# The last projection by seven half-size products instead of eight, half of its weight sums made by accumulating DMAs

## The chip, the cores and the metric

The kernel runs on one core of a Trainium2 chip. The metric is the device time of one execution in microseconds (us); less is better. The kernel before has a median of 1404.72 us over 3 runs (1404.39 to 1404.82).

## The reference, cut to what matters

A decoder trunk of two layers over 512 tokens with 2048 features, all in float32. The second layer (pooling mixer) ends in the projection that is changed:

```python
def _odd_mixer(h, w_in, c_w, c_b, c_scale, w_out):
    p = h @ w_in
    v, z = jnp.split(p, 2, axis=-1)
    pooled = _causal_pool_means(v) - v
    ...
    g = jnp.einsum("bsgc,gcd->bsgd", g, c_w) + c_b
    y = g.reshape(bsz, s, W_C) * c_scale
    return (y * jax.nn.silu(z)) @ w_out        # (512 x 2048) @ (2048 x 2048)
...
x = x + _rmsnorm(y, o_norm_post[i])
```

## The kernel before, in words

Every float32 operand of a matrix product is split in a rounded part (`hi`, type float32r) and a rest (`lo`), and a product is three matmuls, hi·hi, hi·lo and lo·hi, 512 columns each (`product`, L417 to L419). The kernel is written out by hand: each engine has its own instruction list, and semaphores alone order them.

Weights come in slabs of 128 x 2048 (1 MB). SyncE (SP) loads a slab into one of two `raw` buffers (`load`, L253) as soon as VectorE (DVE) has made the rest of the slab before the last. ScalarE (ACT) rounds it into `w_hi` (L650), DVE subtracts and writes `w_lo` (L909), each into one of four slots; `split_ahead` does it three slabs ahead of the TensorE (PE), and a slot is free when PE has counted the slab four places earlier in `slab_done`. `lo_ready` counts finished slabs.

The end of the second layer goes like this. (1) Four groups of channels are mapped by a 512 x 512 matrix each (`o_cw`, one slab per group). GpSimd (POOL) makes the rests of the pooled tiles (L404), ACT rounds them (L849); DVE adds the bias and multiplies by the gate (`group`, L1197), ACT rounds the gated tiles (`mapped_rounded`, L873), DVE makes their rests (L1079). Even groups use PSUM banks 0 to 3, odd ones banks 4 to 7. (2) The last projection: 4 blocks of 512 output columns, each 4 slabs (4 feature tiles of 128 each); 4 tiles of 128 tokens per slab, so 16 products or 48 matmuls a slab, 768 matmuls in all. The tokens are the stationary operand, the weights move. (3) Behind a block ACT squares each token tile's bank with a sum (`y_squares`, L786) and DVE multiplies it by the gain into `rows` (L1105). The last block is done token tile by token tile; then DVE reduces the sums, POOL raises them to -1/2 (L375), DVE scales and adds the residual (L1128), and SP stores (L312, L315). The residual rows `x_mid` and the gain `o_post` are loaded ahead of the second block.

Of the kernel before, what the change touches and what calls it, by code (L numbers as in the profile page):

```python
# [20 lines left out]

# [49 lines left out]

A_X, A_B, A_C, A_Z, B_VAL, B_GATE, B_Z = (n * W_A for n in range(7))
# [13 lines left out]
def build(nc, x, x_t, vec, e_post, e_in, e_out, o_pre, o_post, o_in, o_cw, o_out, out):  # L86
    ctx = ExitStack()
    with ctx:
        def sb(name, shape, dt=F32):
            return ctx.enter_context(nc.sbuf_tensor(name, shape, dt))  # L90
# [4 lines left out]

        h_hi = sb("h_hi", [P, KT, T], F32R)
# [20 lines left out]
        diagonals = sb("diagonals", [P, TT, P])  # L117
# [9 lines left out]
        silu_z = scratch[:, :].rearrange("p (j t) -> p j t", j=KT)  # L127

# [67 lines left out]
        out_ready = sem("out_ready")  # L196

# [41 lines left out]
        def _(sp):  # L239
# [69 lines left out]
            token_major_loads(o_out, AT_O2, ((gain_post, o_post),), x_mid, 2 * KT)  # L309
            for t in range(TT - 1):  # L310
                sp.wait_ge(out_ready, 4 * t + 4)
                sp.dma_start(out[t * P:(t + 1) * P, :], tok[:, t, :]).then_inc(out_stored, 16)  # L312
            for j in range(4):
                sp.wait_ge(out_ready, 4 * (TT - 1) + j + 1)
                sp.dma_start(out[(TT - 1) * P:, j * T:(j + 1) * T],  # L315
                             part4(tok[:, TT - 1, :], j)).then_inc(out_stored, 16)
            sp.wait_ge(out_stored, 16 * (TT - 1 + 4))
# [3 lines left out]
        def _(pool):  # L321
# [84 lines left out]

            powers(POST1, TT)
# [3 lines left out]
        def _(pe):  # L411
# [231 lines left out]
        def _(act):  # L643
# [222 lines left out]

            def mapped_rounded(g):
                for m in range(4):
                    j = 4 * g + m
# [3 lines left out]
                    nc.scalar.activation(h_hi[:, j, :], rows[:, j, :], ACT.Copy)\  # L873
                        .then_inc(u_hi_ready, 1)

            for g in range(NG):
                if g > 0:
                    pooled_rounded(g)
                split_ahead(AT_O1C, g)
                if g > 0:  # L880
                    mapped_rounded(g - 1)
            mapped_rounded(NG - 1)

            post_sets = [POST1 + t for t in range(TT)]
            blocks(AT_O2, 1, post_sets)
            for t in range(TT):
                y_squares(t, AT_O2 + NBLK - 1, NBLK - 1, 1, post_sets, NBLK - 1)
                if t in (1, 2):

                    act.wait_ge(out_ready, 4 * t)  # L890
                    act.dma_start(resid[(t + 1) % 2], x_mid[(t + 1) * P:(t + 2) * P, :])\
                        .then_inc(resid_loaded[(t + 1) % 2], 16)
# [3 lines left out]
        def _(dve):  # L896
# [295 lines left out]
            def group(g):  # L1192
# [8 lines left out]
                for j in range(4 * g, 4 * g + 4):  # L1201
                    u_rest(j, KT + j)
# [48 lines left out]
```

## Time and profile before

| what | value |
|---|---|
| median of 3 runs | 1404.72 us |
| the profiled execution: its span | 1402.8 us |
| TensorE matmul busy | 1377.8 us, 98% |
| VectorE busy | 698.9 us, 50% |
| ScalarE busy | 384.5 us, 27% |
| GpSimd busy | 109.9 us, 8% |
| last projection, first matmul to the last bank's square | 1220.60 to 1395.07 us |
| granted TensorE clock | full speed in all 40 slices |

The span runs from the first to the last instruction of one profiled execution; the device time of the runs is about 1.9 us above it. Matmuls overlap in the profile (each is shown for some 390 ns, while the next starts some 227 ns after it), so the rate is read from a count in a stretch and not from one duration.

### The profile page before, as it was taken

How to read it: one execution, taken by the hardware profiler on the slowest of the kernel's cores; microseconds unless marked ns; L12 is line 12 of the kernel's file. 1: busy time of each engine (PE TensorE's matmuls, PEld its weight loads, DVE VectorE, ACT ScalarE, POOL GpSimd, SP SyncE). 2: the span in 40 equal slices, each digit the busy share in tenths (PEclk: the TensorE clock that was granted, in tenths of full speed). 3: DMA queues.
4: the chain of work that ended last, by engine and by line, in shares of the span. 5: the costliest groups of instructions: out<-in, count | busy, mean ns of one | idle time of the engine just before them, and what ended most of it. 6: DMA issues, size and time to landing. Idle time of an engine off the chain costs nothing.

```text
span 1402.8 us, 16146 instructions
## 1 busy us (share of the span) xinstructions
PE 1377.8 (98%) x6466; PEld 1156.4 (82%) x6466; DVE 698.9 (50%) x767; ACT 384.5 (27%) x413; POOL 109.9 (8%) x101
## 2 busy tenths in 40 slices
PE   5999999999999999999999999999999999999997
PEld 4988888888888888888888899888888888888886
DVE  7588888888753223334332585444522222722333
ACT  5332233222222122223321353222222223512220
POOL 5100000000008200000000000000000003400000
PEclk9999999999999999999999999999999999999999
DMA  8243333434243333333422364333333322262204
GB/s 245 61 111 95 94 112 98 120 90 112 71 127 90 109 90 91 90 105 137 178 90 95 119 205 121 92 99 105 96 90 100 109 90 90 64 236 90 90 30 180
DMA packets 208307, 154.82 MB, mean 110 GB/s; under 512 B 2576, under 2 KB 187024, under 8 KB 205968
## 3 DMA queue, kind: packets, MB, share of 16 engines
q1 hardware_dynamic: 207120, 145.94, 35.1%
q10 hardware_dynamic: 1152, 8.39, 1.6%
q8 instruction: 25, 0.41, 0.1%
q14 instruction: 10, 0.08, 0.0%
HBM read 145.93 MB, written 8.39 MB: 110 GB/s over the span
## 4 chain that ended last, share of the span: by engine, by line
PE 96%; DVE 2%; issue 1%; DMA 0%; ACT 0%; DVEq 0%; POOLq 0%; POOL 0%
PE bank L417 32%; PE bank L418 32%; PE bank L419 32%; DVE h_lo L971 1%; DVE scratch L977 1%; PE bank L447 0%; DVE rows L964 0%; DMA rows<-x_t 0%; DVE diagonals L942 0%; DVE w_lo L986 0%; DVE rows L1128 0%; PE bank L476 0%; PE bank L485 0%; ACT scratch L682 0%; PE bank L545 0%
## 5 line engine op out<-in xcount | busy, mean ns | idle before, releaser
L417 PE MATMUL bank<-h_hi,w_hi 128*128 128x512 f32 (+1 forms) x1600 | 597.3, 373 | 4.9 <-DVE h_lo L971 4.8
L418 PE MATMUL bank<-h_lo,w_hi 128*128 128x512 f32 (+1 forms) x1600 | 595.3, 372 | 0.0
L419 PE MATMUL bank<-h_hi,w_lo 128*128 128x512 f32 (+1 forms) x1600 | 595.3, 372 | 0.0
L909 DVE TENSOR_TENSOR w_lo<-raw,w_hi 128x2048 fp32r<-128x2048 f32 x121 | 280.3, 2317 | 215.7 <-ACT w_hi L650 194.7
L417 PEld LDWEIGHTS bank<-h_hi,w_hi 128*128 128x128 f32 x1600 | 301.4, 188 | 59.3 <-issue 4.5
L419 PEld LDWEIGHTS bank<-h_hi,w_lo 128*128 128x128 f32 x1600 | 301.4, 188 | 52.6
L418 PEld LDWEIGHTS bank<-h_lo,w_hi 128*128 128x128 f32 x1600 | 301.4, 188 | 52.4 <-issue 0.5
L650 ACT ACTIVATE w_hi<-raw 128x2048 fp32r<-128x2048 f32 x122 | 233.3, 1912 | 238.2 <-PE bank L419 189.6
L1004 DVE SCALAR_TENSOR_TENSOR rows<-shifted,vecs,rows 128x512 f32 x256 | 198.0, 776 | 42.2 <-ACT rows L720 10.9
L417 PE MATMUL bank<-w_hi,h_hi 128*128 128x512 f32 x512 | 199.5, 390 | 0.0
L419 PE MATMUL bank<-w_hi,h_lo 128*128 128x512 f32 x512 | 199.3, 389 | 0.0
L418 PE MATMUL bank<-w_lo,h_hi 128*128 128x512 f32 x512 | 199.3, 389 | 0.0
L417 PEld LDWEIGHTS bank<-w_hi,h_hi 128*128 128x128 f32 x512 | 96.1, 188 | 20.7
L419 PEld LDWEIGHTS bank<-w_hi,h_lo 128*128 128x128 f32 x512 | 96.1, 188 | 20.0
L418 PEld LDWEIGHTS bank<-w_lo,h_hi 128*128 128x128 f32 x512 | 96.1, 188 | 19.6
L1170 DVE TENSOR_TENSOR shifted<-shifted 128x512 f32<-128x512 f32 x40 | 27.7, 693 | 84.7 <-ACT shifted L840 83.9
L1189 DVE TENSOR_SCALAR scratch<-scratch,vecs x16 | 7.8, 488 | 109.9 <-ACT scratch L861 109.9
L404 POOL TENSOR_TENSOR h_lo<-rows,h_hi 128x512 fp32r<-128x512 f32 x16 | 29.1, 1847 | 350.7 <-ACT h_hi L849 350.7
L786 ACT ACTIVATE shifted<-bank 128x512 bf16<-128x512 f32 x32 | 19.1, 597 | 102.0 <-PE bank L419 102.0
L861 ACT ACTIVATE scratch<-bank 128x512 f32 (+1 forms) x16 | 9.6, 598 | 133.0 <-PE bank L419 133.0
L738 ACT ACTIVATE scratch<-bank 128x512 f32<-128x512 f32 x16 | 9.6, 598 | 131.2 <-PE bank L419 131.2
L375 POOL TENSOR_TENSOR rstd<-meansq,minus_half 128x1 f32<-128x1 f32 x12 | 6.5, 542 | 495.0 <-DVE meansq L920 495.0
(79 smaller groups left out, 442.6 us busy)
## 6 DMA issues: line engine op xcount, KB each, us to landing
raw<-e_in SPq DMA_DIRECT2D x54, 1024.0 KB, 5.6
raw<-o_in SPq DMA_DIRECT2D x32, 1024.0 KB, 6.0
raw<-e_out SPq DMA_DIRECT2D x16, 1024.0 KB, 5.1
raw<-o_out SPq DMA_DIRECT2D x16, 1024.0 KB, 5.0
rows<-x_t SPq DMA_DIRECT2D x8, 512.0 KB, 6.5
x_mid<-rows ACTq DMA_DIRECT2D x4, 1024.0 KB, 4.8
raw<-o_cw SPq DMA_DIRECT2D x4, 1024.0 KB, 5.3
out<-rows SPq DMA_DIRECT2D x3, 1024.0 KB, 3.9
```

The source lines that it names most:

```text
L404: nc.gpsimd.tensor_tensor(h_lo[:, k, :], rows[:, k, :], f32(h_hi[:, k, :]), ALU.subtract).then_inc(pool_lo_ready, 1)
L417: nc.tensor.matmul(dst, w[0], m[0], start=first, stop=False)
L418: nc.tensor.matmul(dst, w[0], m[1], start=False, stop=False)
L419: return nc.tensor.matmul(dst, w[1], m[0], start=False, stop=last)
L650: nc.scalar.activation(w_hi[:, slot, :], raw[:, slot % RAW, :], ACT.Copy)\
L738: nc.scalar.activation(sz[buf], bank[q][:, :], ACT.Silu)\
L786: nc.scalar.activation(junk_y[t], bank[t][:, :], ACT.Square, accum_out=sumsq[:, sets[t], bass.ds(nb, 1)])\
L909: nc.vector.tensor_tensor(w_lo[:, slot, :], raw[:, slot % RAW, :], f32(w_hi[:, slot, :]), ALU.subtract)\
L971: nc.vector.tensor_tensor(h_lo[at], rows[at], f32(h_hi[at]), ALU.subtract)\
L977: nc.vector.reduce_sum(x_partial[:, j, :], x_sq[:, j, :, :].rearrange("p k t -> p t k"), AX.X)\
L1004: ins = nc.vector.scalar_tensor_tensor(out=dst, in0=row[:, at:at + T], scalar=tap(name, c, width, j), in1=dst, op0=ALU.mult, op1=ALU.add)
L1170: link(nc.vector.tensor_tensor(dst[:, PAD:], src[:, PAD:], src[:, PAD - step:PAD - step + T], ALU.add))
```

## The change

The 512 x 2048 by 2048 x 2048 product is cut in halves on all three sides (tokens, features, output columns) and computed by seven half products in Winograd's form of Strassen's scheme. With A the gated activations (A11, A12 for the first 256 tokens, A21, A22 for the others, by halves of the features) and B the weights, four operands are sums of A quarters, four are sums of B quarters, and the results C are sums of products, made partly by accumulating in PSUM and partly by DVE.

A step `s` is a slab of 1 MB as before (4 feature tiles x 512 columns), but serves only 2 tiles of 128 tokens: 8 products or 24 matmuls. There are 7 products x 2 column blocks (`nb`) x 2 slabs = 28 steps, 672 matmuls (`seventh`, `four`). Steps 0 to 3 are A11·B11, 4 to 7 A12·B21, 8 to 11 (A21-A22)·T1, 12, 13, 16, 17 a sum of A quarters with T2, 14, 15, 18, 19 a sum with B22, 20 to 23 a sum with T3, 24 to 27 A22·T4. T1 to T4 are sums of weight quarters.

The weights now pass nine buffers of 1 MB: `c0` to `c3` hold the running sums, `b0` to `b4` pieces (`raw`, the whole of `scratch` in quarters, parts of `h_hi` and `h_lo` that are free, and the space of `shifted`). 24 pieces are loaded instead of 16. Of the 16 weight sums, eight are made by DVE (`add`), and eight by accumulating DMAs, issued by POOL, which read one SBUF buffer and add it to another (`add_by_dma`): T1 (steps 8 to 11) and T3 (steps 20 to 23). A load into a buffer waits for the step that last read it (`low_done`) and for the accumulating DMA that read it (`t1_added`, `t3_added`). `high(s)` and `low(s)` are the split of step s by ACT and DVE; the step's slot is free when PE has counted step s-4. Gated tiles are written so that each quarter of A is contiguous; `a_high` and `a_low` split a quarter's 2048 columns (or half of it for the first two).

The results: ACT copies finished banks to SBUF (`first_sums`, `first_products`, `second_sums`), DVE combines them with others in PSUM (`c11`, `c12`, `c22`), and PE may not start a later step on the same bank before: steps 8 and 10 wait for `c11(0)` and `c11(1)`, steps 20 and 22 for `c12(0)` and `c12(1)`, steps 24 and 26 for `c22(0)` and `c22(1)`. The gain and the four residual tiles are now loaded at the end, when steps 24 to 27 have been split; the gains and the additions of tiles 0 and 1 and of half of tiles 2 and 3 are all in that end.

```diff
--- before.py
+++ after.py
...
+SPLIT_FROM = ("c0", "c1", "c2", "c3", "b0", "b1", "b2", "b3", "c0", "c1", "c2", "c3",
+              "c0", "c1", "b3", "b4", "c2", "c3", "b0", "b1", "b2", "b3", "b4", "b0",
+              "c0", "c1", "c2", "c3")
+ADDED_FROM = {8: "b4", 9: "b0", 10: "b1", 11: "b2", 12: "b3", 13: "b4", 16: "b0", 17: "b1",
+              20: "b3", 21: "b4", 22: "b0", 23: "b1", 24: "b1", 25: "b2", 26: "b3", 27: "b4"}
...
+        buffers = {"c0": raw[:, 0, :], "c1": raw[:, 1, :], "c2": scratch[:, 0:SLAB],
+                   "c3": scratch[:, SLAB:2 * SLAB], "b0": scratch[:, 2 * SLAB:3 * SLAB],
+                   "b1": scratch[:, 3 * SLAB:], "b2": spare2[:, :], "b3": spare3[:, :],
+                   "b4": spare4[:, :]}
...
-            token_major_loads(o_out, AT_O2, ((gain_post, o_post),), x_mid, 2 * KT)
...
+            def piece(w, dst, kh, nh, nb, p):
+
+                src = w.rearrange("(k p) n -> p k n", p=P)[
+                    :, kh * KH + p * 4:kh * KH + (p + 1) * 4,
+                    nh * NH + nb * T:nh * NH + (nb + 1) * T]
+                sp.dma_start(buffers[dst].rearrange("p (k c) -> p k c", c=T), src)\
+                    .then_inc(piece_loaded[dst], 16)
...
+            low_done(6)
+            piece(o_out, "b2", 0, 1, 1, 1)
+            low_done(7)
+            piece(o_out, "b3", 1, 1, 0, 0)
+            sp.wait_ge(t1_added[0], 16)
+            piece(o_out, "b4", 1, 1, 0, 1)
...
+            sp.wait_ge(t3_added[0], 16)
+            low_done(14)
+            piece(o_out, "b3", 0, 1, 0, 1)
+            sp.wait_ge(t3_added[1], 16)
+            low_done(15)
+            piece(o_out, "b4", 0, 1, 1, 0)
+            sp.wait_ge(t3_added[2], 16)
+            low_done(18)
+            piece(o_out, "b0", 0, 1, 1, 1)
+            sp.wait_ge(t3_added[3], 16)
+            low_done(19)
+            piece(o_out, "b1", 1, 0, 0, 0)
+            low_done(20)
+            piece(o_out, "b2", 1, 0, 0, 1)
+            low_done(21)
+            piece(o_out, "b3", 1, 0, 1, 0)
+            low_done(22)
+            piece(o_out, "b4", 1, 0, 1, 1)
+            low_done(24)
...
+            def add_by_dma(dst, src, news):
+
+                nc.gpsimd.dma_start(buffers[dst], buffers[src], accum_op=ALU.add)\
+                    .then_inc(news, 16)
+
+            pool.wait_ge(lo_ready, LAST + 1)
+            pool.wait_ge(piece_loaded["b4"], 16)
+            add_by_dma("c0", "b4", t1_added[0])
...
+            pool.wait_ge(lo_ready, LAST + 4)
+            pool.wait_ge(piece_loaded["b2"], 32)
+            add_by_dma("c3", "b2", t1_added[3])
+            pool.wait_ge(piece_loaded["b2"], 48)
+            pool.wait_ge(piece_loaded["b3"], 32)
+            add_by_dma("b2", "b3", t3_added[0])
+            pool.wait_ge(piece_loaded["b3"], 48)
+            pool.wait_ge(piece_loaded["b4"], 32)
+            add_by_dma("b3", "b4", t3_added[1])
+            pool.wait_ge(piece_loaded["b4"], 48)
+            pool.wait_ge(piece_loaded["b0"], 48)
+            add_by_dma("b4", "b0", t3_added[2])
...
-            with pe.Fori(0, NBLK - 1) as nb:
-                token_major(nb + AT_O2, 1, KT)
-            token_major_last(AT_O2 + NBLK - 1, 1, lambda t: None)
...
+            def four(dst, slot, s, tt, fresh):
+
+                p = s % 2
+                for kk in range(4):
+                    last = product(dst, form(slot, 4 * p + kk, tt), weights(s % SLOTS, kk, T),
+                                   fresh and p == 0 and kk == 0, p == 1 and kk == 3, True)
+                return last
+
+            def seventh(s, dst, slot, forms, fresh, ready):
+
+                for p in range(2):
+                    pe.wait_ge(lo_ready, LAST + s + p + 1)
+                    pe.wait_ge(a_lo_ready, forms[p])
+                    for tt in range(2):
+                        if p == 0:
+                            ready(tt)
+                        last = four(dst(tt), slot, s + p, tt, fresh)
+                        if p == 1 and tt == 0:
+                            last.then_inc(chain_done, 1)
+                    last.then_inc(slab_done, 1)
+
+            for nb in range(2):
+                seventh(2 * nb, lambda tt: y_bank(nb, tt), SLOT_A, (1, 2), True,
+                        lambda tt: pe.wait_ge(bank_free[2 * nb + tt], AT_O2 + 2))
+            for nb in range(2):
+                seventh(4 + 2 * nb, lambda tt: w_bank(nb, tt), SLOT_B, (3, 4), True,
+                        lambda tt: pe.wait_ge(bank_free[4 + 2 * nb + tt],
+                                              uses4(4 + 2 * nb + tt, "map", 2) + 1))
+            for nb in range(2):
+                seventh(8 + 2 * nb, lambda tt: w_bank(nb, tt), SLOT_C, (5, 5), True,
+                        lambda tt: pe.wait_ge(c11_ready, 2 * nb + tt + 1))
+            for nb in range(2):
+                seventh(12 + 4 * nb, lambda tt: y_bank(nb, tt), SLOT_A, (6, 6), False,
+                        lambda tt: pe.wait_ge(c11_ready, 2 * nb + tt + 1))
+                seventh(14 + 4 * nb, lambda tt: w_bank(nb, tt), SLOT_B, (7, 7), False,
+                        lambda tt: pe.wait_ge(w1_ready, 2 * nb + tt + 1))
+            for nb in range(2):
+                seventh(20 + 2 * nb, lambda tt: y_bank(nb, tt), SLOT_C, (8, 8), False,
+                        lambda tt: pe.wait_ge(c12_ready, 2 * nb + tt + 1))
+            for tt in range(2):
+                for nb in range(2):
+                    pe.wait_ge(c22_ready, 2 * nb + tt + 1)
+                    for p in range(2):
+                        s = 24 + 2 * nb + p
+                        if tt == 0:
+                            pe.wait_ge(lo_ready, LAST + s + 1)
+                            pe.wait_ge(a_lo_ready, 9)
+                        last = four(y_bank(nb, tt), SLOT_A, s, tt, False)
+                        if tt == 1:
+                            last.then_inc(slab_done, 1)
+                        elif p == 1:
+                            last.then_inc(chain_done, 1)
 
...
+            high_t1(9)
+            high_t1(10)
+            for tt in range(2):
+                act.wait_ge(c11_ready, tt + 1)
+                square(c_block(C11, 0, tt), tt, 0, tt)
+            high_t1(11)
+            act.wait_ge(a_summed, 3)
+            act.wait_ge(slab_done, done(LAST + 8))
+            a_high(SLOT_B, 0, quarter(A12))
+            high_added(12)
+            for tt in range(2):
+                act.wait_ge(c11_ready, 2 + tt + 1)
+                square(c_block(C11, 1, tt), tt, 1, 2 + tt)
+            high_added(13)
...
+            second_sums(1)
+            act.wait_ge(slab_done, done(LAST + 18))
+            a_high(SLOT_A, 0, quarter(A22))
+            high_t3(22)
+            high_t3(23)
+            high_added(24)
+            for tt in range(2):
...
+            low(9)
+            c11(0)
+            low(10)
+            add(12, 2)
+            low(11)
+            c11(1)
+            a_low(SLOT_B, 0, quarter(A12), 7)
+            low(12)
+            add(13, 2)
+            low(13)
+            low(14)
+            add(16, 3)
+            low(15)
...
+            low(22)
+            add(24, 4)
+            low(23)
+            c12(1)
+            add(25, 4)
+            low(24)
+            add(26, 4)
+            low(25)
+            c22(0)
+            add(27, 4)
+            low(26)
+            dve.wait_ge(c_squared, 8)
+            mean_square(POST1)
+            mean_square(POST1 + 1)
+            low(27)
+            c22(1)
+            dve.wait_ge(final_gain_loaded, 16)
+            for t in range(2):
+                gain(c_half(C11, t), c_half(C11, t), 0, NH, 4)
...
```

Three places in the instruction lists. POOL's list behind the mapping, before:

```order
L404 TENSOR_TENSOR h_lo<-rows,h_hi 128x512 x16
L375 TENSOR_TENSOR rstd<-meansq,minus_half 128x1 x4
```

and with the change (raw is c0 or c1, scratch is c2, c3, b0 or b1, spare_70 is b2, spare_71 is b3, spare_72 is b4; what is left of the arrow is added to):

```order
L559 TENSOR_TENSOR h_lo<-rows,h_hi 128x512 x16
L564 DMA raw<-spare_72 128x2048
L564 DMA raw<-scratch 128x2048
L564 DMA scratch<-scratch 128x2048
L564 DMA scratch<-spare_70 128x2048
L564 DMA spare_70<-spare_71 128x2048
L564 DMA spare_71<-spare_72 128x2048
L564 DMA spare_72<-scratch 128x2048
L564 DMA scratch<-scratch 128x2048
L530 TENSOR_TENSOR rstd<-meansq,minus_half 128x1 x4
```

POOL had nothing between the last rest and the norm; eight accumulating DMAs stand there now, in order, each behind waits for its two buffers.

DVE's list during the mapping of groups 0 to 2, before (L909 is a slab's rest, L1197 a group's gating, L1079 its rests):

```order
L1197 SCALAR_TENSOR_TENSOR rows<-bank,vecs,scratch 128x512 x4
L1079 TENSOR_TENSOR h_lo<-rows,h_hi 128x512 x4
L909 TENSOR_TENSOR w_lo<-raw,w_hi 128x2048
L1197 SCALAR_TENSOR_TENSOR rows<-bank,vecs,scratch 128x512 x4
L1079 TENSOR_TENSOR h_lo<-rows,h_hi 128x512 x4
```

and with the change (L1601 `low`, L1588 `a_low`, L1576 the gating):

```order
L1576 SCALAR_TENSOR_TENSOR rows<-bank,vecs,scratch 128x2x256 x4
L1601 TENSOR_TENSOR w_lo<-raw,w_hi 128x2048
L1588 TENSOR_TENSOR h_lo<-rows,h_hi 128x1024
L1576 SCALAR_TENSOR_TENSOR rows<-bank,vecs,scratch 128x2x256 x4
L1601 TENSOR_TENSOR w_lo<-scratch,w_hi 128x2048
```

The rests of group 0, now one instruction over 1024 columns, stand behind the slab and so directly ahead of the gating of group 1; before they stood ahead of the slab.

DVE's list around steps 21 to 26, with the change (L1609 is `add`, L1630 `c12`, L1638 `c22`; before, there was one L909 per slab here and, every fourth slab, four L1105):

```order
L1588 TENSOR_TENSOR h_lo<-rows,h_hi 128x2048
L1601 TENSOR_TENSOR w_lo<-spare_72,w_hi 128x2048
L1609 TENSOR_TENSOR raw<-raw,scratch 128x2048
L1601 TENSOR_TENSOR w_lo<-scratch,w_hi 128x2048
L1630 TENSOR_TENSOR rows<-bank,rows 128x512 x2
L1609 TENSOR_TENSOR raw<-raw,spare_70 128x2048
L1601 TENSOR_TENSOR w_lo<-raw,w_hi 128x2048
L1609 TENSOR_TENSOR scratch<-scratch,spare_71 128x2048
L1601 TENSOR_TENSOR w_lo<-raw,w_hi 128x2048
L1638 TENSOR_TENSOR rows<-rows,bank 128x512 x2
L1609 TENSOR_TENSOR scratch<-scratch,spare_72 128x2048
L1601 TENSOR_TENSOR w_lo<-scratch,w_hi 128x2048
```

Step 22 of PE waits for the L1630 pair, and ahead of that pair stand a sum from a piece (`add(24)`, from b1) and the rest of step 23.

## Rows read from the trace of the kernel before

**Rows 1.** The page: span, busy time, and the 40 slices.
```profile
span 1402.8 us, 16146 instructions
...
PE 1377.8 (98%) x6466; PEld 1156.4 (82%) x6466; DVE 698.9 (50%) x767; ACT 384.5 (27%) x413; POOL 109.9 (8%) x101
...
PEclk9999999999999999999999999999999999999999
...
```

**Rows 2.** Who waited for whom, 1190 to 1403 us.
```profile
...
DVE w_lo L909 <- ACT w_hi L650: 85.9, 15, 8.6
ACT w_hi L650 <- PE bank L419: 72.4, 11, 9.0
...
```

**Rows 3.** Busy time by stretch, through the last projection and behind it.
```profile
...
core 0: us, PE busy (x) PEld busy (x) DVE busy (x) ACT busy (x) POOL busy (x), PEclk, DMA share, GB/s
...
1221.00:1395.00 174.00, 174.00 (x767) 143.52 (x766) 53.80 (x54) 37.25 (x47) 1.62 (x3) 1.00 0.34 121
...
```

**Rows 4.** Groups of instructions by shape, 1208 to 1403 us.
```profile
...
L419 PE MATMUL bank<-w_hi,h_lo 128*128 128x512 f32 x256 | 99.7, 389 | 0.0
...
L909 DVE TENSOR_TENSOR w_lo<-raw,w_hi 128x2048 fp32r<-128x2048 f32 x14 | 32.1, 2292 | 79.5 <-ACT w_hi L650 74.2 <-DMA scratch<-o_post 5.3
L650 ACT ACTIVATE w_hi<-raw 128x2048 fp32r<-128x2048 f32 x14 | 26.8, 1914 | 77.5 <-PE bank L419 64.7 <-DMA raw<-o_out 12.8
...
L786 ACT ACTIVATE shifted<-bank 128x512 bf16<-128x512 f32 x16 | 9.6, 597 | 60.0 <-PE bank L419 60.0
...
L1105 DVE TENSOR_TENSOR rows<-bank,scratch 128x512 f32 x12 | 8.1, 692 | 16.6 <-ACT shifted L786 16.6
...
```

**Rows 5.** Instructions in order of time around the last mapping: POOL, ACT, DVE, PE.
```profile
...
1207.18 8.16 POOL L404 TENSOR_TENSOR h_lo<-rows,h_hi 128x512 fp32r<-128x512 f32 x4 [2.75 <-ACT h_hi L849]
...
1203.97 2.61 ACT L873 ACTIVATE h_hi<-rows 128x512 fp32r<-128x512 f32 x4 [3.02 <-DVE rows L1197]
1206.49 2.18 ACT L849 ACTIVATE h_hi<-rows 128x512 fp32r<-128x512 f32 x4
...
1200.99 2.29 DVE L909 TENSOR_TENSOR w_lo<-raw,w_hi 128x2048 fp32r<-128x2048 f32 x1 [3.55 <-ACT w_hi L650]
1203.20 2.72 DVE L1197 SCALAR_TENSOR_TENSOR rows<-bank,vecs,scratch 128x512 f32<-128x512 f32 x4
...
1220.60 0.39 PE L417 MATMUL bank<-w_hi,h_hi 128*128 128x512 f32 x1
...
```

**Rows 6.** A 1024-wide ACT group, whole span.
```profile
...
L682 ACT ACTIVATE scratch<-rows 128x1024 f32<-128x1024 f32 x8 | 8.4, 1049 | 4.3 <-DMA rows<-x_t 4.3
...
```

**Rows 7.** DMA issues by line, 1220 to 1403 us, median to landing.
```profile
...
raw<-o_out SPq DMA_DIRECT2D x12, 1024.0 KB, 5.1
out<-rows SPq DMA_DIRECT2D x3, 1024.0 KB, 3.9
scratch<-x_mid SPq DMA_DIRECT2D x2, 1024.0 KB, 8.1
...
```

**Rows 8.** Landing of the one load that L253 issued from 1225 to 1228 us.
```profile
...
DMA to landing us min/median/max: 11.1/11.1/11.1
```

**Rows 9.** Busy time by stretch while four transfers were in flight.
```profile
...
1231.00:1239.00 8.00, 8.00 (x37) 6.61 (x36) 2.29 (x1) 0.22 (x1) 0.00 (x0) 1.00 1.02 409
...
```

**Rows 10.** The end in order of time: ACT, DVE, POOL.
```profile
...
1395.07 0.60 ACT L786 ACTIVATE shifted<-bank 128x512 bf16<-128x512 f32 x1 [10.19 <-PE bank L419]
...
1396.05 0.68 DVE L1105 TENSOR_TENSOR rows<-bank,scratch 128x512 f32<-128x512 f32 x1
1396.85 2.74 DVE L1128 SCALAR_TENSOR_TENSOR rows<-rows,rstd,scratch 128x512 f32<-128x512 f32 x4
...
1396.22 0.54 POOL L375 TENSOR_TENSOR rstd<-meansq,minus_half 128x1 f32<-128x1 f32 x1 [10.34 <-DVE meansq L920]
```

**Rows 11.** Granted clock behind the last matmul.
```profile
...
1397.00:1399.00 2.00, 0.00 (x0) 0.00 (x0) 2.00 (x4) 0.00 (x0) 0.00 (x0) 0.69 0.28 102
1399.00:1401.00 2.00, 0.00 (x0) 0.00 (x0) 0.59 (x1) 0.00 (x0) 0.00 (x0) 0.50 1.07 343
...
```

More of the change, by code:

```diff
@@ L886, in _ @@
[L886 to L892, printed above, removed]
+                first = g % 2 * QW // 2
+                a_high(SLOT_A if g < 2 else SLOT_B, first,
+                       quarter(A11 if g < 2 else A12, first, QW // 2))
@@ new lines, in a_low, with gated_low @@
+            def a_low(slot, first, src, n):
+                width = src.shape[-1]
+                at = slot * QW + first
+                dve.wait_ge(a_hi_ready, n)
+                nc.vector.tensor_tensor(form_lo[:, at:at + width], src,
+                                        f32(form_hi[:, at:at + width]), ALU.subtract)\
+                    .then_inc(a_lo_ready, 1)
+            def gated_low(g):
+                first = g % 2 * QW // 2
+                a_low(SLOT_A if g < 2 else SLOT_B, first,
+                      quarter(A11 if g < 2 else A12, first, QW // 2), g + 1)
@@ new lines, in gain, with finished @@
+            def gain(dst, src, first, width, squares):
+                dve.wait_ge(c_squared, squares)
+                nc.vector.tensor_tensor(dst, src, buffers["c0"][:, first:first + width],
+                                        ALU.mult).then_inc(c_gained, 1)
+            def finished(t, dst, first, width, gains):
+                dve.wait_ge(c_gained, gains)
+                resid = buffers[("c1", "c2", "c3", "b2")[t]]
+                nc.vector.scalar_tensor_tensor(
+                    out=dst, in0=dst, scalar=rstd[:, POST1 + t:POST1 + t + 1],
+                    in1=resid[:, first:first + width], op0=ALU.mult, op1=ALU.add)\
+                    .then_inc(out_ready, 1)
@@ new lines, in _ @@
+            dve.wait_ge(z_scaled, KT)
+            split_ahead(AT_O1C, 0)
+            low(0)
+            group(0)
+            low(1)
+            gated_low(0)
+            group(1)
+            low(2)
+            gated_low(1)
+            group(2)
+            gated_low(2)
+            group(3)
+            low(3)
+            gated_low(3)
+            for b in range(8):
+                dve.wait_ge(bank_free[b], uses4(b, "map", 2) + 1 if b >= 4 else AT_O2 + 2)
+            nc.vector.tensor_tensor(quarter(A21), quarter(A21), quarter(A22), ALU.subtract)\
+                .then_inc(a_summed, 1)
@@ new lines, in _ @@
+            low(9)
[11 more added lines that the diff above has]
+            low(15)
+            a_low(SLOT_C, 0, quarter(A21), 8)
+            low(16)
+            add(17, 3)
+            low(17)
+            low(18)
+            low(19)
+            c12(0)
+            low(20)
```

361 lines of the change are left out of this document (320 added, 41 removed).

## The prediction

> **What bounds the kernel now.** I read the page first: TensorE is busy 1377.8 of 1402.8 us, at full clock in every slice, VectorE half of the time, ScalarE 27%, GpSimd 8% [rows 1]. Then who waits for whom near the end: VectorE waits for ScalarE's rounding, and that for TensorE to give a slot back [rows 2]; no row has TensorE waiting for anybody there. The stretch of the last projection says the same: 174.00 us, 767 matmuls, busy for all of it [rows 3]. So in this stage only the number of matmuls counts, 174.00/767 = 0.2269 us each, and everything beside it has room: VectorE 53.8 us busy, ScalarE 37.3. The question is whether the room is enough for what the change puts there.
>
> **The change part by part.** I count time t from the first matmul of the last projection, at 1220.60 us [rows 5]. A step of 24 matmuls is 5.44 us, so step s starts at 5.44 s if nothing stalls.
>
> *Removed matmuls.* 768 - 672 = 96, times 0.2269: **-21.8 us**. Form and shape stay, and the rate is that of a stretch in which one bank is also fed many times in a row.
>
> *The mapping before it.* The 1024-wide rest (half of a 2.29 us one [rows 4], 1.15) now stands ahead of group 1's gating. That gating ended at 1203.20 + 2.72 = 1205.92 [rows 5], now 1207.07. ScalarE rounds the group behind it, now in one piece of 1.05 us [rows 6], since it waits for all four tiles: 1208.2. Then one pooled tile, 2.18/4 = 0.55, and GpSimd's rest of it, 8.16/4 = 2.04: 1210.9. TensorE starts group 3 48 matmuls before 1220.60, at 1209.7; before, that rest was there at 1207.18 + 2.04 = 1209.2, a cover of 0.5. **+1.2** (0.5 to 2).
>
> *VectorE and ScalarE in the steps.* A step needs 1.91 of ScalarE and 2.29 of VectorE [rows 4]. VectorE gets 8 sums of weights, 4 of activations and 5 rests of quarters, all at 2.29 (same width, two SBUF inputs), and 12 combinations at 0.69 [rows 4]. With 24 rests of slabs that is 41 x 2.29 + 8.3 = 102 us of 152. ScalarE: 24 x 1.91, 5 x 1.91, 12 copies and 16 squares of 0.6 to 0.8 [rows 4], some 77. Neither is the bound on average; the order is what can hurt, below.
>
> *The accumulating DMA.* Nothing in the trace adds in a DMA. From below: a plain store of 1 MB takes 3.9 us, a plain load 5.1 from issue to landing [rows 7]. With four transfers in flight the engines moved 409 GB/s [rows 9], 2.56 us per MB: call it a pass. The addition reads two buffers, so one pass more than a load: 5.1 + 2.56 = 7.7. GpSimd also has to issue it, and its smallest operation takes 0.54 [rows 10]. I take A = 8.5 us, nearest to the load. From above: three transfers one behind the other, 3 x 5.1 = 15.3; the load behind three others took 11.1 [rows 8].
>
> The Trainium skill ("Collectives: The Full Stack", on why ReduceScatter is half of AllGather) says that a DMA addition is slow through its two source reads and not through the adder, about half the rate of a copy. No row here shows an addition. Doubling the load row, A would be 10.2, and the sum below 1393 instead of 1388.
>
> *First chain, the sums for steps 8 to 11.* Step 4 is split when step 0 is done (5.4) and VectorE has gone through group 3 and one sum of activations: some 11. Only then is b0 free, its reload lands at 16, and the second accumulation starts; the third and fourth follow behind the rests of steps 5 and 6 and a load each. From t = 16 until the fourth lands there are six loads and three accumulations, 6 + 3 x 2 = 12 passes: 30.7 us, so it lands at L = 47. Step 10 may start (54.4) when `c11(1)` is done, and ahead of that stand the rounding and the rest of step 11 and 1.1 us more: L + 5.3 = 52.3. No stall, with 2 us left. Before, this wait was on the banks alone and long over.
>
> *Second chain, the sums for steps 20 to 23.* The rest of step 14 frees b3. VectorE's list is in order, so behind L come: rounding and rest of step 11, `c11(1)`, a rest of a quarter, rest of 12, sum 13, rounding of 13, two copies, rounding and rest of 14, together 20.2 us. Then, each waiting for the last: load b3, add, load b4, add, load b0, add, load b1. The last is needed because `add(24)` stands ahead of `low(23)`, and that ahead of `c12(1)`, for which TensorE waits with step 22 at 119.7. So it is ready at L + 20.2 + 4 x 5.1 + 3A + 5.3 + some 1 us of hand-overs = L + 3A + 46.9, and the stall is **L + 3A - 73**. With L = 47 and A = 8.5: -0.5, so **0**. Each microsecond of A costs 3 from there on. Queued behind `c12(1)` on VectorE are the last three sums and four rests, for which TensorE waits in turn.
>
> *VectorE behind step 22.* Between `c12(1)` and `c22(1)` stand 7 x 2.29 + 4 x 0.69 + two mean squares, 19.5 us, and TensorE needs `c22(1)` after 2 steps and 2 half steps, 16.3. With half a microsecond of slack **+3** (0 to 3.2).
>
> *The end.* The last tile's path is as before: square, mean square, power, four additions of 0.68 and a store [rows 10]. But ten 1024-wide gains and additions of the other tiles, some 1.3 each, and tile 2's own 4.3 stand ahead, 17.3 us against TensorE's 16.3 behind `c22(1)`, and gain and residuals are loaded just before. **+1** (0 to 5).
>
> *Sum.* 1402.8 - 21.8 + 1.2 + 0 + 3 + 1 = 1386.2 of span, and 1.9 around it (1404.7 less 1402.8): **1388 us**.
>
> **The rivals.**
> (a) *The sums come somewhat late*: A from 9.5 to 12. For: the two chains hang on it, and loads and accumulations share the engines. Against: in the second chain only one transfer is in flight at a time. A = 10.2, a load twice, gives 47 + 30.6 - 73 = 4.6 and 1393; A = 12 with L = 16 + 3 x 12 = 52 gives 15, 1403.
> (b) *Slower than before, through the accumulations alone*: they run at a rate of their own, below that of the transfers. With A = 15.3 the three lie behind each other from t = 16, L = 62, the stall of both chains together is 62 + 45.9 - 73 = 35, and the time 1388 + 35 = 1423. It decides from some A = 12 on, where the stalls reach 16.6. For: no row bounds the adder, and a long stall costs more than itself, since the granted clock was 0.69 in the stretch from 1.9 us after TensorE's last matmul and 0.50 after that (1.2 GHz) [rows 11], and matmuls then take twice the time. Against: only the pessimistic end of the bound gets there.
> (c) *The gain goes at the end*: gain, four residual tiles and 4 MB of output share the engines in the last 25 us. Nine passes are 23 us; if the residuals land late, +5 to +8, 1393 to 1396. Against: the stores begin only when additions are done, and 5 passes fit in the 16 us.
> (d) *Nothing changes*: stalls happen to equal 17 us, 1404 to 1405.
>
> The Trainium skill ("DMA: Bandwidth & Descriptors", "Issuing engines are not separate DMA queues") says that DMAs from GpSimd and SyncE share the same 16 engines. The two SyncE loads of `x_mid` beside others took 8.1 instead of the 5.1 of a load alone [rows 7], both issued by SyncE; a GpSimd DMA is in no row. It speaks for (a).
>
> **How the numbers follow.** Forecast (A up to 9.5, 1384 to 1392): 0.47. (a): 0.15. (c): 0.05. (b): 0.30. (d): 0.03. Measurement can tell about 0.2%, 2.8 us, from no change. Faster: 0.47 + 0.15 + 0.05 = 0.67, less 0.01 at (a)'s edge, 0.66; same 0.03 + 0.01 = 0.04; slower 0.30. The low end is all stalls at nothing but the mapping's: 1404.7 - 21.8 + 0.6 = 1383.5. The top takes in (b) to A = 15.3 and a little of the clock, 1426; beyond lie perhaps 15 of 100. The likeliest case alone: 1384 to 1392.
>
> **What would show it.** 672 matmuls in the last projection at 0.227. Issue to landing of the accumulating DMAs: near 8.5 when alone (the last four), 12 to 18 for the second to fourth. TensorE's waits: about 1 us on GpSimd's rests before group 3, none before step 10, 0 to 1 before step 22, 3 before step 26. Wrong is the prediction if the last four accumulations take over 11 us, if TensorE waits before steps 8 to 11, or if the span's end lies over 10 us behind the last matmul.

## The result, and the profile after

The changed kernel takes 1384.0 us (median of 4 runs, 1383.7 to 1384.9) against 1404.77 for the kernel before beside it: the ratio is 0.9853, 95% interval 0.9839 to 0.9867. That is 20.8 us less. The forecast was 1388, with 1383.5 to 1426 as the range.

The page of the changed kernel, its span, busy times, clock and the queue of the accumulating DMAs:

```profile
span 1382.2 us, 15947 instructions
...
PE 1356.9 (98%) x6370; PEld 1139.2 (82%) x6370; DVE 765.1 (55%) x784; ACT 415.7 (30%) x430; POOL 112.8 (8%) x109
...
PEclk9999999999999999999999999999999999999999
...
q0 software_dynamic: 1152, 8.39, 3.1%
...
```

The span is 20.6 us shorter than before [rows 1], TensorE is still 98% busy at full clock, and TensorE's matmul instructions are 96 fewer. VectorE went from 698.9 to 765.1 us, ScalarE from 384.5 to 415.7. The eight accumulating DMAs moved 8.39 MB. The stretch of the last projection:

```profile
...
core 0: us, PE busy (x) PEld busy (x) DVE busy (x) ACT busy (x) POOL busy (x), PEclk, DMA share, GB/s
1221.88:1374.20 152.32, 152.32 (x673) 125.94 (x671) 122.34 (x81) 73.04 (x73) 7.67 (x10) 1.00 0.75 232
...
```

152.3 us for some 672 matmuls, 0.2266 each, instead of 174.0 for 767 [rows 3]: the rate did not change. VectorE is busy 122.3 us of it (53.8 before), ScalarE 73.0, and the DMA engines 75%. Nothing of that reaches TensorE, whose list of waits from 1180 us on is one line:

```profile
...
PE bank L602 <- issue: 1.1, 1, 1.1
```

The list counts a wait from the end at which a matmul is shown (0.39 us behind its start); from start to start, less one matmul of 0.2266, this one is 1.26. It stands before mapping group 3, 48 matmuls ahead of the last projection. Here is how it comes about, VectorE, ScalarE, GpSimd and TensorE in turn:

```profile
...
1200.96 3.02 DVE L1601 TENSOR_TENSOR w_lo<-raw,w_hi 128x2048 fp32r<-128x2048 f32 x1 [5.95 <-ACT w_hi L1128]
1203.90 1.21 DVE L1588 TENSOR_TENSOR h_lo<-rows,h_hi 128x1024 fp32r<-128x1024 f32 x1
1205.04 2.71 DVE L1576 SCALAR_TENSOR_TENSOR rows<-bank,vecs,scratch 128x512 f32<-128x512 f32 x4
...
1207.87 1.06 ACT L1113 ACTIVATE h_hi<-rows 128x1024 fp32r<-128x1024 f32 x1 [6.93 <-DVE rows L1576]
1208.83 2.17 ACT L1091 ACTIVATE h_hi<-rows 128x512 fp32r<-128x512 f32 x4
...
1209.52 7.08 POOL L559 TENSOR_TENSOR h_lo<-rows,h_hi 128x512 fp32r<-128x512 f32 x4 [7.69 <-ACT h_hi L1091]
...
1209.41 0.39 PE L606 MATMUL bank<-h_hi,w_lo 128*128 128x512 f32 x1
1210.90 0.47 PE L602 MATMUL bank<-h_hi,w_hi 128*128 128x512 f32 x1 [1.10 <-issue]
...
```

The gating of group 1 ends at 1207.75 instead of 1205.92 [rows 5], since a rest of 1.21 us stands ahead of it and the slab's rest took 3.02 instead of 2.29; ScalarE's piece ends at 1208.93, GpSimd starts group 3's rests at 1209.52 instead of 1207.18, and TensorE, which would have gone on at 1209.64, goes on at 1210.90: 1.26 us. With 96 x 0.2266 = 21.8 less, that is 20.5 of the 20.6 us.

GpSimd's start came 2.34 us later and TensorE waited only 1.26, because the first of the four rests, the one that TensorE needs first, was shorter. Changed kernel, then GpSimd and VectorE in the kernel before:

```profile
...
1209.52 1.27 POOL L559 TENSOR_TENSOR h_lo<-rows,h_hi 128x512 fp32r<-128x512 f32 x1 [7.69 <-ACT h_hi L1091]
...
1207.18 2.29 POOL L404 TENSOR_TENSOR h_lo<-rows,h_hi 128x512 fp32r<-128x512 f32 x1 [2.75 <-ACT h_hi L849]
...
1205.83 2.49 DVE L1079 TENSOR_TENSOR h_lo<-rows,h_hi 128x512 fp32r<-128x512 f32 x4
...
```

In the kernel before, this rest began while VectorE made rests of its own, until 1208.32, and ended 1.15 us behind them, at 1209.47. In the changed kernel nothing of VectorE ran beside it. The other way round, GpSimd's rest from 1200.55 to 1201.83 was under way when VectorE's slab rest began at 1200.96, and that one took 0.73 us longer. These rows look as if, of two such rests at the same time, the one that began first kept its usual time and held up the other; no run here varies it.

GpSimd's issues of the accumulating DMAs, four for T1 and two of the four for T3:

```profile
...
1216.55 1.05 POOL L564 DMA_DIRECT2D raw<-spare  x1
1240.14 0.87 POOL L564 DMA_DIRECT2D raw<-scratch  x1 [22.54 <-DMA scratch<-o_out]
1251.53 0.86 POOL L564 DMA_DIRECT2D scratch<-scratch  x1 [10.52 <-DMA scratch<-o_out]
1254.29 0.88 POOL L564 DMA_DIRECT2D scratch<-spare  x1 [1.91 <-DMA spare<-o_out]
1278.51 0.86 POOL L564 DMA_DIRECT2D spare<-spare  x1 [23.34 <-DMA spare<-o_out]
...
1318.53 0.88 POOL L564 DMA_DIRECT2D scratch<-scratch  x1 [11.64 <-DMA scratch<-o_out]
...
```

and their times from issue to landing:

```profile
...
scratch<-scratch POOLq DMA_DIRECT2D x2, 1024.0 KB, 9.5
spare<-spare POOLq DMA_DIRECT2D x2, 1024.0 KB, 7.1
...
raw<-spare POOLq DMA_DIRECT2D x1, 1024.0 KB, 8.3
raw<-scratch POOLq DMA_DIRECT2D x1, 1024.0 KB, 8.4
scratch<-spare POOLq DMA_DIRECT2D x1, 1024.0 KB, 14.9
spare<-scratch POOLq DMA_DIRECT2D x1, 1024.0 KB, 7.0
...
```

The first two lines put two additions each together: the 9.5 stands for T1's third, 12.0, and T3's fourth, 7.0; the 7.1 for T3's first two, 7.2 and 7.0. One alone (the four of T3) takes 7.0 to 7.2 us; 8.3 to 8.4 beside loads; 12.0 for the third of T1; 14.9 for the fourth of T1, which shares the engines with the third and with loads. It is issued at 1254.29 and lands at 1269.2, t = 47.3 from the first matmul of the projection (1221.88). The end of the second chain and the two combinations on VectorE:

```profile
...
1330.59 2.29 DVE L1609 TENSOR_TENSOR raw<-raw,scratch 128x2048 f32<-128x2048 f32 x1 [0.85 <-DMA scratch<-o_out]
1332.89 2.29 DVE L1601 TENSOR_TENSOR w_lo<-scratch,w_hi 128x2048 fp32r<-128x2048 f32 x1
1335.10 1.28 DVE L1630 TENSOR_TENSOR rows<-bank,rows 128x512 f32<-128x512 f32 x2
...
1354.65 2.29 DVE L1601 TENSOR_TENSOR w_lo<-scratch,w_hi 128x2048 fp32r<-128x2048 f32 x1 [2.48 <-ACT w_hi L1128]
1356.86 1.28 DVE L1638 TENSOR_TENSOR rows<-rows,bank 128x512 f32<-128x512 f32 x2
...
```

`c12(1)` ends its first half at 1335.7, 5.8 us before step 22 starts (1221.88 + 119.6 = 1341.5). `c22(1)` has its first half ready at 1357.5; step 26 starts at 1357.9. Ahead of it VectorE was idle for 2.48 us: it waited for ScalarE, and that for TensorE to free the slot of step 23:

```profile
...
1352.70 1.92 ACT L1128 ACTIVATE w_hi<-scratch 128x2048 fp32r<-128x2048 f32 x1 [2.30 <-PE bank L606]
```

The end is the old one [rows 10]: the last square at 1374.40, then mean square, gain, four additions, stores, 7.8 us from that square to the end of the span, as before.

```profile
...
1374.40 0.60 ACT L1162 ACTIVATE junk<-bank 128x512 bf16<-128x512 f32 x1 [4.75 <-PE bank L606]
...
1375.12 0.16 DVE L1297 TENSOR_REDUCE total<-sumsq 128x1 f32<-128x4 f32 x1 [0.72 <-ACT junk L1162]
...
1376.20 2.74 DVE L1651 SCALAR_TENSOR_TENSOR rows<-rows,rstd,spare 128x512 f32<-128x512 f32 x4
```

### The profile page after: what moved, and what is told of

It is laid out like the page before. It is cut to its first block, busy times and chain, and to the rows that moved or that the text cites. A ratio compares the mean times of both kernels' runs of the same rounds, so it can differ in the third digit from the quotient of the medians.

```text
span 1382.2 us, 15947 instructions
## 1 busy us (share of the span) xinstructions
PE 1356.9 (98%) x6370; PEld 1139.2 (82%) x6370; DVE 765.1 (55%) x784; ACT 415.7 (30%) x430; POOL 112.8 (8%) x109
## 3 DMA queue, kind: packets, MB, share of 16 engines
q0 software_dynamic: 1152, 8.39, 3.1%
HBM read 154.32 MB, written 8.39 MB: 118 GB/s over the span
## 4 chain that ended last, share of the span: by engine, by line
PE 97%; DVE 2%; DMA 0%; issue 0%; ACT 0%; SPq 0%; DVEq 0%; ACTq 0%
PE bank L602 32%; PE bank L604 32%; PE bank L606 32%; DVE h_lo L1349 1%; PE bank L635 1%; DMA rows<-x_t 0%; DVE rows L1342 0%; DVE scratch L1355 0%; DVE diagonals L1320 0%; DVE w_lo L1364 0%; DVE rows L1651 0%; PE bank L664 0%; PE bank L673 0%; ACT scratch L924 0%; SPq L321 0%
## 5 line engine op out<-in xcount | busy, mean ns | idle before, releaser
L1287 DVE TENSOR_TENSOR w_lo<-raw,w_hi 128x2048 fp32r<-128x2048 f32 x105 | 243.6, 2320 | 123.7 <-ACT w_hi L892 108.9
L892 ACT ACTIVATE w_hi<-raw 128x2048 fp32r<-128x2048 f32 x106 | 202.7, 1912 | 152.7 <-PE bank L606 117.1
L1382 DVE SCALAR_TENSOR_TENSOR rows<-shifted,vecs,rows 128x512 f32 x256 | 198.0, 776 | 42.2 <-ACT rows L962 10.9
L602 PE MATMUL bank<-w_hi,h_hi 128*128 128x512 f32 x480 | 187.0, 390 | 0.0
L606 PE MATMUL bank<-w_hi,h_lo 128*128 128x512 f32 x480 | 186.8, 389 | 0.0
L604 PE MATMUL bank<-w_lo,h_hi 128*128 128x512 f32 x480 | 186.8, 389 | 0.0
L602 PEld LDWEIGHTS bank<-w_hi,h_hi 128*128 128x128 f32 x480 | 90.1, 188 | 19.1
L606 PEld LDWEIGHTS bank<-w_hi,h_lo 128*128 128x128 f32 x480 | 90.1, 188 | 18.9
L604 PEld LDWEIGHTS bank<-w_lo,h_hi 128*128 128x128 f32 x480 | 90.1, 188 | 18.2
L1082 ACT ACTIVATE shifted<-bank 128x512 f32<-128x512 f32 x16 | 9.6, 598 | 122.1 <-PE bank L606 122.1
L971 ACT ACTIVATE rows<-shifted,vecs 128x512 f32 x8 | 5.8, 724 | 125.0 <-DVE shifted L1407 125.0
```

The costliest lines, as they stand in the source:

```text
L602: nc.tensor.matmul(dst, w[0], m[0], start=first, stop=False, skip_group_check=goes_on)
L604: nc.tensor.matmul(dst, w[0], m[1], start=False, stop=False, skip_group_check=goes_on)
L892: nc.scalar.activation(w_hi[:, slot, :], raw[:, slot % RAW, :], ACT.Copy)\
L1082: nc.scalar.activation(v_row[:, PAD:], bank[q][:, :], ACT.Copy)\
L1287: nc.vector.tensor_tensor(w_lo[:, slot, :], raw[:, slot % RAW, :], f32(w_hi[:, slot, :]), ALU.subtract)\
L1382: ins = nc.vector.scalar_tensor_tensor(out=dst, in0=row[:, at:at + T], scalar=tap(name, c, width, j), in1=dst, op0=ALU.mult, op1=ALU.add)
```

## The experiments

Ten runs: eight altered kernels, one of them twice, and the changed kernel once more. Where one changes a sum, its expectation says which.

### 1 and 8. The rest of group 0 behind the gating of group 1

```diff
             low(1)
-            gated_low(0)
             group(1)
+            gated_low(0)
```

> The changed kernel, but VectorE's rest of group 0 stands behind the gating of group 1 and not ahead of it. My theory: the one wait of TensorE, 1.26 us before mapping group 3, comes from that place; it goes, and the time falls by 1.2 us, 1384.0 to 1382.8. Rival: the wait comes from VectorE's longer slab rests beside GpSimd (3.02 instead of 2.29 us); then at least 0.5 us of it stays, and the time falls by less than 0.8.

Measured: 1383.41 us (1382.6 to 1384.54), the wait gone but for 0.14 us. The medians' distance of 0.6 says little with this spread, so both versions ran once more on one chip.

> The changed kernel once more, to stand on the same chip beside the next one: 1384.0 and the wait of 1.26 us before mapping group 3.

> The version with VectorE's rest of group 0 behind the gating of group 1 once more, on the same chip as the changed kernel: the wait is gone (at most 0.2 us), and the median is 1.0 to 1.3 us below the changed kernel's. If the two medians agree within 0.3 us, the time is given back elsewhere.

Measured: the changed kernel 1384.13 us (1383.19 to 1384.68), the other 1382.93 (1382.77 to 1383.78), ratios to the kernel before 0.9852 and 0.9846. That is 1.2 us, with ranges that overlap a little; the profiled executions say the same, with spans of 1382.2 and 1381.0 and the first matmul of the projection at 1221.93 and 1220.77. VectorE's list in the second:

```profile
...
1200.94 3.03 DVE L1601 TENSOR_TENSOR w_lo<-raw,w_hi 128x2048 fp32r<-128x2048 f32 x1 [5.95 <-ACT w_hi L1128]
1203.89 2.71 DVE L1576 SCALAR_TENSOR_TENSOR rows<-bank,vecs,scratch 128x512 f32<-128x512 f32 x4
1206.53 1.21 DVE L1588 TENSOR_TENSOR h_lo<-rows,h_hi 128x1024 fp32r<-128x1024 f32 x1
```

The slab's rest still takes 3.03 us, and the wait is gone all the same but for 0.16. So the place of the rest costs the 1.2 us; the longer slab rest alone does not. This is the fastest version of the study.

### 2. All sums on VectorE

```diff
-            add_by_dma("c0", "b4", t1_added[0])
...
+            def add_piece(dst, src, waits, news):
+                for name, count in waits:
+                    dve.wait_ge(piece_loaded[name], 16 * count)
+                nc.vector.tensor_tensor(buffers[dst], buffers[dst], buffers[src], ALU.add)\
+                    .then_inc(news, 1)
```

The eight sums stand in VectorE's list behind `low(3)`, `low(6)`, `low(8)`, `c11(0)`, `low(15)`, `low(17)`, `low(19)` and `low(20)`.

> The changed kernel with all 16 weight sums on VectorE, no accumulating DMA. My theory: TensorE alone bounds the stage and VectorE has room for 8 x 2.29 = 18.3 us more (102 to 120 of 152); waits of 0 to 4 us where a sum stands in the way, so 1384 to 1388. Rival: VectorE is so near its limit that the DMAs are what makes the gain; then waits of 8 us or more, 1392 and above.

Measured: 1385.69 us (1385.23 to 1385.99), ratio 0.9863 (0.9848 to 0.9878). TensorE's wait beside that before mapping group 3:

```profile
...
PE bank L572 <- DVE rows L1600: 0.9, 1, 0.9
```

One wait more, before step 8, of 0.9 (1.1 from start to start). The medians differ by 1.7 us from the changed kernel's 1384.0; of this the wait explains 1.1, and in the profiled executions another 0.7 lies ahead of 1210 us, where nothing is changed (the matmul before mapping group 3 starts at 1210.13 instead of 1209.41). So what the accumulating DMAs are shown to be worth is 1.1 us, through the order of VectorE's list; the seven products give the rest without them.

### 3. The additions of T3 twice

```diff
+            twice = t3_added
...
                 nc.gpsimd.dma_start(buffers[dst], buffers[src], accum_op=ALU.add)\
                     .then_inc(news, 16)
+                if news in twice:
+                    pool.wait_ge(news, 16)
+                    nc.gpsimd.dma_start(buffers[dst], buffers[src], accum_op=ALU.add)\
+                        .then_inc(news, 16)
```

SyncE and ScalarE wait for both runs of a sum (32 instead of 16).

> The changed kernel with each of the four accumulating DMAs of T3 (steps 20 to 23) run twice, one behind the other, so that this sum counts its second operand twice. My theory: in the chain load, add, load, add each addition counts three times in full; 3 x 7.0 = 21 us more, less 5.1 us of slack before step 22, 15.9 us of wait there, and 3 us before step 26: 1403, waits before no other step. Rival: the additions are off the chain (the loads alone set it); then 0 to 5 us, 1384 to 1389.

Measured: 1408.52 us (1407.82 to 1410.14), slower than the kernel before (1.0029, 1.0019 to 1.0039). One new wait, before step 22:

```profile
...
PE bank L608 <- DVE rows L1636: 21.4, 1, 21.4
...
```

21.4 us and not 15.9, and none before step 26. Two rows tell where the difference comes from. GpSimd, the second addition of T3 and its repetition:

```profile
...
1299.79 0.85 POOL L566 DMA_DIRECT2D spare<-spare  x1 [12.44 <-DMA spare<-o_out]
1307.16 0.87 POOL L570 DMA_DIRECT2D spare<-spare  x1 [6.51 <-DMA spare<-spare]
...
```

The second is issued at 1299.79 instead of 1293.73 (0.8 of it is older than the projection in this execution): I had counted three additions in the chain, but the first, done twice, outlasts the rest of step 14 that covers it. And the clock behind the wait, in stretches (the seventh of the numbers without brackets is the granted clock):

```profile
...
1364.00:1367.00 3.00, 3.00 (x7) 2.40 (x8) 3.00 (x3) 1.54 (x5) 0.00 (x0) 0.50 0.76 277
1367.00:1372.00 5.00, 5.00 (x20) 3.99 (x19) 5.00 (x3) 1.72 (x2) 0.00 (x0) 0.87 0.45 144
...
```

After the wait the granted clock is 0.50, the 1.2 GHz level, and back at 1.00 from 1369 us on; a matmul starts every 0.43 us for 4.4 us. From step 22 on TensorE takes 34.6 us and not 32.4 to its last matmul, so the wait costs 2.2 us more than itself. This also gives VectorE the time that it would have lacked before step 26: `c22(1)` has its first half ready 18.1 us behind the start of step 22, and at full clock step 26 would start after 16.3.

### 10. Only the last three additions of T3 twice

The same edit with `twice = t3_added[1:]`.

> The changed kernel with the last three additions of T3 run twice and the first once; their operand counts twice. In the run with all four twice the wait before step 22 was 21.6 us, 5.7 more than I had worked out. My theory: the first addition has some 3 us of cover (the rest of step 14 frees b3 later), and twice it outlasts that by 5 us; with it single the wait is 3 x 7.4 less 5.5 of slack, 16.7 us, and the time 1403 to 1404. Rival: the additions simply take longer with their second run; then the wait stays above 20.

Measured: 1402.86 us (1402.09 to 1403.73), ratio 0.9987 (0.9977 to 0.9997).

```profile
...
PE bank L608 <- DVE rows L1636: 16.2, 1, 16.2
...
```

16.2 us where 16.7 was expected, and a time just below the expected 1403 to 1404: the first addition was the missing part, and the others count in full.

### 5. The additions of T3 twice, the sum for step 24 behind the combination

```diff
             low(22)
-            add(24, 4)
             low(23)
             c12(1)
+            add(24, 4)
```

> As the kernel with the additions of T3 run twice (which waited 21.6 us before step 22), but VectorE's sum for step 24 stands behind the combination for which step 22 waits, and not two places ahead of it. The sum still counts its second operand twice. My theory: the chain to step 22 ends with load b1, sum 24, rest of 23, combination; without the load and the sum 10.3 us behind the last addition become 4.9, so the wait falls by some 5.4 us, to 16; what was put off comes back in part before step 26 (up to 4 us), so 1403 to 1407 against 1408.5. Rival: the chain ends with the last addition and the load is beside it; then the wait stays within 1 us of 21.6.

Measured: 1406.5 us (1404.97 to 1408.9), ratio 1.0009 (1.0000 to 1.0019).

```profile
...
PE bank L608 <- DVE rows L1636: 16.2, 1, 16.2
PE bank L608 <- DVE rows L1644: 2.6, 1, 2.6
...
```

The wait before step 22 fell from 21.4 to 16.2 us, so the load of b1 and the sum are part of the chain; 2.6 us came back before step 26, as the sum now stands between the two combinations. The profiled execution is the slowest of the ten (1408.9). One thing in it I had not looked for: the short second wait was followed by a longer stretch at the lower clock than the long first one, 6.1 us against 3.1:

```profile
...
1359.00:1362.00 3.00, 2.93 (x7) 2.40 (x8) 2.77 (x3) 0.25 (x1) 0.00 (x0) 0.50 1.05 391
1379.80:1386.00 6.20, 6.19 (x15) 4.84 (x16) 6.20 (x6) 1.90 (x6) 0.00 (x0) 0.50 0.97 398
...
```

### 4. The additions of T1 twice

The edit of experiment 3 with `twice = t1_added`.

> The changed kernel with each of the four accumulating DMAs of T1 (steps 8 to 11) run twice, so that this sum counts its second operand twice. My theory: in that stretch the engines' throughput counts, in passes of 2.56 us per MB: 6 more passes put the landing of the fourth from t = 47.4 to 62.8, and the wait, 13.7 us, is before step 10, with none or little more before step 22: 1398. Rival: latency of the serial additions and not throughput; each costs 7 us alone, the fourth lands 7 us later, 5 us of wait before step 10, 1389.

Measured: 1410.8 us (1409.86 to 1411.26), ratio 1.0041 (1.0025 to 1.0056), beyond both theories. TensorE waited twice, 5.1 us before step 8 and 17.3 before step 10, together:

```profile
...
PE bank L608 <- DVE rows L1629: 22.1, 2, 17.1
...
1272.65 0.85 POOL L570 DMA_DIRECT2D scratch<-scratch  x1 [14.39 <-DMA scratch<-scratch]
1273.19 1.20 POOL L566 DMA_DIRECT2D scratch<-spare  x1
...
```

The two GpSimd rows show why: the repetition for c2 is issued at 1272.65, and the first addition for c3 at 1273.19, instead of 1254.29. GpSimd's list is in order, and my added wait held up every addition behind it. So this run tells nothing on throughput against latency.

### 9. Only the fourth addition of T1 twice

The same edit with `twice = t1_added[3:]`, so that nothing is queued behind it.

> The changed kernel with only the fourth addition of T1 (c3 from b2, for step 11) run twice; step 11's weights count that operand twice. GpSimd has nothing to issue behind it for 20 us, so no other addition is put off. My theory: it lands 7 to 8 us later, c11(1) is ready 2 us before step 10 in the changed kernel, so TensorE waits 5 to 6 us before step 10, nowhere else (step 22 has 5 us of slack and is shifted as well), and 1 to 2 us are lost to the lower clock behind the wait: 1390 to 1392. Rival: the wait of 17 us in the run with all four twice came from the engines' throughput; then this one costs 3 us or less.

Measured: 1394.46 us (1393.83 to 1395.1), ratio 0.9928 (0.9912 to 0.9945).

```profile
...
PE bank L608 <- DVE rows L1629: 8.2, 1, 8.2
...
DMA to landing us min/median/max: 10.3/10.3/10.3
```

One wait, before step 10, 8.2 us. It is larger than the 5 to 6 that I expected, and the time than the 1390 to 1392, because the repetition took 10.3 us beside loads, and not 7 to 8: 10.3 + 0.2 less 2.2 of slack is 8.3. The rival (3 us or less) is out: the fourth landing decides step 10. No wait before step 22.

### 6. Copies instead of additions

```diff
-                nc.gpsimd.dma_start(buffers[dst], buffers[src], accum_op=ALU.add)\
+                nc.gpsimd.dma_start(buffers[dst], buffers[src])\
```

> The changed kernel with the eight DMAs that GpSimd issues copying and not adding, so that T1 and T3 are only their second operands. What the addition costs over a copy: by the two-read theory the copies alone in flight take one pass of 2.5 us less than the 7.0 of the additions, 4.5 us. By the rival theory (the adder or GpSimd's issue takes the time) they take 6 to 7. Either way the additions are hidden in the changed kernel, and the time stays at 1384 within 1 us.

Measured: 1384.45 us (1383.72 to 1385.61), ratio 0.9858 (0.9843 to 0.9873).

```profile
...
spare<-spare POOLq DMA_DIRECT2D x2, 1024.0 KB, 4.6
...
scratch<-spare POOLq DMA_DIRECT2D x1, 1024.0 KB, 10.9
...
```

A copy alone takes 4.5 to 4.8 us where an addition takes 7.0 to 7.2: some 2.4 us more, near one pass of 2.56 [rows 9]. Of it 0.33 is GpSimd's issue, 0.53 instead of 0.86. A copy does without the second read and without the adding, so this run gives the price of both together. The fourth landed after 10.9 us instead of 14.9. The time stayed: in the changed kernel the additions are hidden.

## Why the prediction was right, point by point

**Removed matmuls, -21.8.** Right: 96 fewer at an unchanged 0.2266.

**The mapping, +1.2.** Right in its place and its path: 1.26 measured, and experiments 1 and 8 take it back. The size is in part luck. VectorE's slab rest took 3.02 instead of 2.29, 0.73 more than the sum had, and GpSimd's rest that counts took 1.27 instead of the mean of 2.04, 0.77 less. The mean was the wrong figure to take: of the four rests in it the first took 2.29 and the last 3.40, both beside work of VectorE, and the other two 1.3 each.

**The accumulating DMA, A = 8.5.** Too high: 7.0 to 7.2 alone. The bottom of my bound (7.7, a load and one pass) was above it too, because a copy between SBUF buffers takes 4.6 us, less than the load's 5.1. The step that failed is "GpSimd also has to issue it": I added 0.8 for that to a row that already has an issue in it; experiment 6 shows 0.33 more than for a copy. The Trainium skill ("Collectives: The Full Stack", why ReduceScatter is half of AllGather) puts the cost of the addition on its two source reads. Experiment 6 agrees as far as it goes, with one pass more, though it can't tell the read from the adding. The halved rate, applied to the whole 4.6 us as I applied it to the load, gives 9.2, and 7.0 was measured: only a part of the time grew.

**First chain, L = 47, no stall.** Right: the fourth landed at t = 47.3, and `c11(1)` was ready 2.2 us before step 10. The agreement within 0.3 us is in part luck: the second addition was issued at 1240.14, t = 18.3 and not 16, as b0's reload took 6.4 us and the hand-overs some more, and from there 29.0 us passed and not the 30.7 of 12 passes. The second took 8.4 us, outside the 12 to 18 that I gave for the second to fourth. With copies the count by passes did about as well: 9 passes from 16.9 give 39.9, measured 40.7. Experiment 9 shows that this landing decides step 10.

**Second chain, stall = L + 3A - 73.** Its links are shown: experiment 10 prices three additions in full, experiment 5 the load and the sum at its end. With the measured L and A (7.05) the formula gives 47.3 + 21.2 - 73 = -4.5, and `c12(1)` was 5.8 us early. One condition was missing: "each waiting for the last" holds for the first addition only once it is 2.7 us longer. It landed at 1285.7, and the load of b3 behind it had to wait for the rest of step 14 until 1288.4; done twice it passed that (experiment 3, 5.2 us more wait than experiment 10).

**VectorE behind step 22, +3.** Not there. The term that failed is this one: it rested on half a microsecond of slack, the -0.5 that A = 8.5 gave, and there were 5.8. Back-to-back, VectorE's operations also start every 2.20 us and not every 2.29. What stands closest to a wait now is something that I had not named: step 26 has 0.4 us left, and not through VectorE's load but through the slot that step 23 frees (rounding 1.92, rest 2.29, combination). In experiments 3 and 10 the slack was gone and still no wait came up before step 26: VectorE needed 18.1 us against 16.3, and the lower clock covered the difference. The 2.6 us of experiment 5 have one sum of 2.2 us more in that stretch.

**VectorE's load.** The 102 us of 152 were 122.3. The count left out the gains and additions of the end (some 17 us), group 3's gating and rests, and the rest of the slab ahead of step 4. It changed nothing, as TensorE never waited for the load on average.

**The end, +1.** Not there: VectorE was 0.7 us ahead when the last square came, 1.18 and 1.24 per 1024-wide operation instead of 1.3, and gain and residuals landed in 4.7 to 7.1 us.

So 1388 less 3, less 1, is the measured 1384; the forecast's case was the right one. The 3 came from a margin that A = 8.5 had eaten up, the 1 from a margin at the end that was there. 1384.0 is at the bottom of "1384 to 1392", where nothing but the mapping's wait is left. Of the rivals, (b) was not met at A = 7.0; that a long wait costs more than itself is shown by the 0.50 clock in experiment 3. (a), (c) and (d) did not happen. The rule of the Trainium skill ("DMA: Bandwidth & Descriptors", "Issuing engines are not separate DMA queues") agrees with the trace: GpSimd's addition took 14.9 us beside SyncE's loads and another addition, 7.0 alone. I gave slower a chance of 0.30 for want of a row; doubling the additions shows how near it was: 7 us more for each and the kernel is slower than before.

What stays open: the way in which VectorE and GpSimd hold each other up in the mapping is read from rows that fit, and no run tests it; and why the lower clock lasted longer behind the shorter wait of experiment 5.

## What to carry to other kernels

Where TensorE is full in every slice, fewer matmuls are worth their number times their rate, as long as the last link of each chain that feeds it is early; write that link as a sum of landings and operations in list order, with its slack, and price a further wait by it. A doubt about one duration multiplies by how often it stands in the chain: here three times. A repeated operation is a good probe for such a chain, but look at what is queued behind the wait that it needs, on the same engine.

## What the runs showed of the hardware

- A DMA that adds 1 MB from SBUF to SBUF took 7.0 to 7.2 us from issue to landing alone, the same as a copy 4.5 to 4.8; GpSimd issued them in 0.86 and 0.53 us.
- With loads, or loads and another addition, in flight an addition took 8.3 to 14.9 us.
- After TensorE's waits of 2.7 to 21.6 us (start to start, experiments 3, 4, 5, 9 and 10) the granted clock was 0.50, and matmuls started every 0.43 us for 2.7 to 6.1 us; the longest such stretch stood behind the shortest of these waits. Waits of 1.26 and 1.1 us (experiment 2) left it at 1.00.
- VectorE's 2048-wide rest took 3.02 us when it began 0.87 us before the end of a GpSimd rest; GpSimd's 512-wide rest took 2.29 us when it began 1.14 us before the end of VectorE's rests, 1.27 when nothing of VectorE ran beside it.
